# Pool matrix of whole numbers, pool channels as a high and a low part, in a two-layer hybrid encoder on one core

## The reference, cut to what matters

```python
for gi, w in enumerate(POOL_WINDOWS):        # 2, 4, 8, 16; one per group of 128 channels
    lo = jnp.clip(t - w // 2, 0, s)
    hi = jnp.clip(t + w - w // 2, 0, s)
    mean = (cs[:, hi, gi] - cs[:, lo, gi]) / (hi - lo)   # cs: cumulative sum over tokens
    outs.append(mean - uf[:, :, gi])
mixed = jnp.einsum('bsgc,gcd->bsgd', pooled, lin)        # one 128x128 map per group
return mixed.reshape(b, s, POOL_WIDTH) * scale
```

## Time and profile before

| | us |
|---|---|
| median of 3 runs | 810.91 (810.03 to 812.22) |
| the profiled execution, its own time | 810.14 |
| its span | 808.3 |
| TensorE busy | 802.1 |
| TensorE weight loads | 658.5 |
| VectorE busy | 572.9 |
| ScalarE busy | 464.0 |
| GpSimd busy | 245.9 |

### The profile page before, as it was taken

The page is one execution under the profiler, slowest core; times in us unless marked ns, Lnnn a source line. Parts: engine busy times, 40 slices in busy tenths (PEclk is TensorE's granted clock), DMA queues, the critical chain, the costliest instruction groups (busy, mean ns, idle before and its releaser), DMA issues.

```text
span 808.3 us, 9803 instructions
## 1 busy us (share of the span) xinstructions
PE 802.1 (99%) x3808; PEld 658.5 (81%) x3808; DVE 572.9 (71%) x684; ACT 464.0 (57%) x534; POOL 245.9 (30%) x206
## 2 busy tenths in 40 slices
PE   8999999999999999999999999999999999999998
PEld 6888877888888888888888887878888888888886
DVE  5899976758685666665379998777686666676551
ACT  5788886574355445544457888856635455355420
POOL 1342623330043444430023325342300444344200
PEclk9999999999999999999999999999999999999999
DMA  9788876864557787686456888675744666776651
GB/s 336 285 242 217 216 225 216 215 223 161 171 211 210 212 220 218 202 244 217 163 203 201 223 226 215 214 222 190 234 156 167 222 207 208 231 234 201 206 205 53
DMA packets 98318, 170.22 MB, mean 211 GB/s; under 512 B 78016, under 2 KB 78176, under 8 KB 80864
## 3 DMA queue, kind: packets, MB, share of 16 engines
q1 hardware_dynamic: 96352, 163.34, 65.5%
q0 software_dynamic: 1632, 6.18, 2.2%
q10 hardware_dynamic: 288, 0.08, 0.0%
HBM read 149.91 MB, written 1.05 MB: 187 GB/s over the span
## 4 chain that ended last, share of the span: by engine, by line
PE 97%; DVE 1%; DMA 1%; ACT 0%; SPq 0%; issue 0%
PE bank L1135 31%; PE bank L1146 30%; PE bank L1137 30%; PE bank L1257 2%; PE bank L1168 1%; PE bank L1234 1%; PE bank L1225 1%; PE bank L1195 1%; DMA x_sb<-in_x_dram 1%; PE bank L1201 0%; DVE w_lo L854 0%; DVE w_lo L860 0%; ACT w_hi L658 0%; DVE scratch L878 0%; DVE aT_lo L887 0%; ACT aT_hi L670 0%
## 5 line engine op out<-in xcount | busy, mean ns | idle before, releaser
L854 DVE TENSOR_TENSOR w_lo<-w_raw,w_hi 128x2048 fp32r<-128x2048 f32 x134 | 314.6, 2349 | 122.5 <-ACT w_hi L658 121.9
L658 ACT ACTIVATE w_hi<-w_raw 128x2048 fp32r<-128x2048 f32 x134 | 256.5, 1915 | 170.3 <-DMA w_raw<-in_stream_dram 170.3
L1135 PE MATMUL bank<-w_hi,aT_hi 128*128 128x512 f32 x832 | 327.6, 394 | 0.2 <-issue 0.2
L1137 PE MATMUL bank<-w_hi,aT_lo 128*128 128x512 f32 x832 | 324.1, 390 | 0.0
L1146 PE MATMUL bank<-w_lo,aT_hi 128*128 128x512 f32 x832 | 223.3, 390 | 0.2 <-DVE w_lo L854 0.2
L1135 PEld LDWEIGHTS bank<-w_hi,aT_hi 128*128 128x128 f32 x832 | 156.2, 188 | 36.6 <-issue 3.4
L1146 PEld LDWEIGHTS bank<-w_lo,aT_hi 128*128 128x128 f32 x832 | 155.6, 188 | 33.0 <-DVE w_lo L854 0.7
L1137 PEld LDWEIGHTS bank<-w_hi,aT_lo 128*128 128x128 f32 x832 | 156.3, 188 | 31.9
L597 POOL COPY halves<-hid 128x512 uint16<-128x512 uint16 x44 | 75.1, 1734 | 4.6 <-DVE hid L1107 4.6
L606 POOL COPY hT_raw<-turned 128x512 uint16<-128x512 uint16 x44 | 33.8, 813 | 134.4 <-DMA turned<-halves 134.4
L1135 PE MATMUL bank<-w_hi,hT_hi 128*128 128x512 f32 x176 | 68.6, 390 | 0.0
(11 more groups left out here) (102 smaller groups left out, 801.6 us busy)
## 6 DMA issues: line engine op xcount, KB each, us to landing
w_raw<-in_stream_dram SPq DMA_DIRECT2D x135, 1024.0 KB, 5.2
bias_sb<-in_b_gate_dram POOLq DMA_DIRECT2D x12, 256.0 KB, 5.7
par<-in_params_dram POOLq DMA_DIRECT2D x3, 384.0 KB, 3.4
w_raw<-in_stream_dram SPq DMA_DIRECT2D x4, 256.0 KB, 5.0
pool_mat<-in_pooling_dram POOLq DMA_DIRECT2D x1, 1024.0 KB, 5.2
out_dram<-x_sb SPq DMA_DIRECT2D x4, 256.0 KB, 3.9
x_sb<-in_x_dram SPq DMA_DIRECT2D x2, 256.0 KB, 4.6
x_sb<-in_x_dram SPq DMA_DIRECT2D x1, 512.0 KB, 7.0
```

Source lines behind the costliest of these rows:

```text
L658: nc.scalar.activation(w_hi[:, j % RING, :, :].rearrange("p k n -> p (k n)"), w_raw[:, j % RING, :, :].rearrange("p k n -> p (k n)"), ACT. ...
L854: nc.vector.tensor_tensor(w[0], w[1], w[2].bitcast(F32), ALU.subtract).then_inc(unit_lo, 1)
L1135: nc.tensor.matmul(o, src[0][:, k, tok], w_hi[:, slot, wk + i, :], start=first and i == 0, stop=False)
L1137: nc.tensor.matmul(o, src[1][:, k, tok], w_hi[:, slot, wk + i, :], start=False, stop=False)
```

## The change

The pool's matrix holds whole numbers: 1 in the window, less the window's count on the diagonal. It is kept as fp32r, cast once by GpSimd in units 7 and 8 of layer 0 from a raw copy that lands in the room of `head_halves`. The pool channels are taken from PSUM as a high part (`u_hi`, ScalarE, unit 13) and a low part (`u_lo`, VectorE, the new `low_pooled`, unit 15), each scaled by `rstd`. A turn is now eight fp32r matmuls in place of four fp32 ones. The turns move to units 16 and 18, z6 moves to banks 2 and 3, and is freed by `low_pooled`. The division by the count comes behind the per-group map: in the mixed turns VectorE multiplies by `pool_scale` and by 1/count in one instruction per group. The reciprocals are a new input, broadcast by one DMA per layer to `inv_counts`, issued by GpSimd in unit 17.

```diff
+U_LOW = 15
...
-    14: [("pool", 0)], 16: [("pool", 1)], 17: [("o", 0)], 20: [("o", 1)], 21: [("mixed", 0)], 23: [("mixed", 1)],
+    16: [("pool", 0)], 17: [("o", 0)], 18: [("pool", 1)], 20: [("o", 1)], 21: [("mixed", 0)], 23: [("mixed", 1)],
...
-        pair(2 if c in (0, 2, 4) else 0, f"z{c}")
+        pair(2 if c in (0, 2, 4, 6) else 0, f"z{c}")
...
-        pool_mat = sb("pool_mat", [P, MT, POOL_G, SEQ])
+        pool_mat = sb("pool_mat", [P, MT, POOL_G, SEQ], F32R)
...
+        pool_raw = head_halves[:, 0:MT * MT * POOL_G * SEQ].bitcast(F32)
...
-            zvu = sb("zvu", [P, MT, VU_W], F32, mixer)
+            zvu = sb("zvu", [P, MT, VU_POOL], F32, mixer)
+            u_hi = sb("u_hi", [P, MT, POOL_W], F32R, mixer)
...
+        inv_counts = zqk[:, 0, 1024:1024 + POOL_G * SEQ].rearrange("p (g n) -> p g n", g=POOL_G)
+        u_lo = [mixT_lo[:, 2:4, :].rearrange("p k n -> p (k n)"), oT_hi[:, 4:6, :].rearrange("p k n -> p (k n)")]
...
+            def load_counts(lay):
+
+                wait_joined(pool, lay, (5, 0))
+                pool.dma_start(inv_counts.rearrange("p g n -> p (g n)"), counts.to_broadcast([P, POOL_G * SEQ])
+                               ).then_inc(counts_loaded, 16)
+
...
-                    pool.dma_start(pool_mat[:, :, :, :].rearrange("p m g n -> p (m g n)"), pooling
+                    pool.dma_start(pool_raw, pooling
                                    ).then_inc(pooling_loaded, 16)
...
+                    if lay == 0 and t in (7, 8):
+                        m = t - 7
+                        pool.wait_ge(pooling_loaded, 16)
+                        for h in range(2):
+                            nc.gpsimd.tensor_copy(
+                                pool_mat[:, m, 2 * h:2 * h + 2, :],
+                                pool_raw.rearrange("p (m g n) -> p m g n", m=MT, g=POOL_G)[:, m, 2 * h:2 * h + 2, :]
+                                ).then_inc(pooling_ready, 1)
+                    if t == 17:
+                        load_counts(lay)
...
+                if c == POOL_CHUNK:
+                    nc.scalar.activation(u_hi[:, m, :], B((f"z{c}", m))[:, :], ACT.Copy, scale=rstd[:, 0, m:m + 1]
+                                         ).then_inc(pool_hi, 1)
+                    return
...
                 if kind == "mixed":
-                    gain = par[:, PR_PS + 2 * i:PR_PS + 2 * i + 2].unsqueeze(2).to_broadcast([P, 2, SEQ])
-                else:
-                    first = (PR_MIX if kind == "mix_x" else PR_FFN) + UK * (i // 2)
-                    gain = par[:, first:first + UK].unsqueeze(2).to_broadcast([P, UK, P])
+                    dve.wait_ge(counts_loaded, lay * 16 + 16)
+                    for h in range(2):
+                        g = 2 * i + h
+                        ins = nc.vector.scalar_tensor_tensor(
+                            scratch[:, NC * (n % 2) + SEQ * h:NC * (n % 2) + SEQ * h + SEQ],
+                            B(name)[:, SEQ * h:SEQ * h + SEQ], par[:, PR_PS + g:PR_PS + g + 1], inv_counts[:, g, :],
+                            ALU.mult, ALU.mult)
+                    free(ins, name)
+                    return
+                first = (PR_MIX if kind == "mix_x" else PR_FFN) + UK * (i // 2)
+                gain = par[:, first:first + UK].unsqueeze(2).to_broadcast([P, UK, P])
...
+            def low_pooled(lay, m):
+
+                for r, k in ((1, 0), (1, 1), (2, 0)):
+                    dve.wait_ge(heads_turned[r][k], (lay + 1) * 16)
+                dve.wait_ge(pool_hi, lay * MT + m + 1)
+                free(nc.vector.scalar_tensor_tensor(u_lo[m], B((f"z{POOL_CHUNK}", m))[:, :], rstd[:, 0, m:m + 1],
+                                                    u_hi[:, m, :].bitcast(F32), ALU.mult, ALU.subtract),
+                     (f"z{POOL_CHUNK}", m))
...
                     for j in splits_at(t):
                         split(lay, j)
+                    if t == U_LOW:
+                        for m in range(MT):
+                            low_pooled(lay, m)
...
-                        pe.wait_ge(pooling_loaded, 16)
+                        pe.wait_ge(pooling_ready, 2 * MT)
                         for m in range(MT):
                             wait_emptied(pe, lay, (f"z{POOL_CHUNK}", m))
                     for g in (2 * i, 2 * i + 1):
                         for m in range(MT):
-                            last = nc.tensor.matmul(b[:, SEQ * (g % 2):SEQ * (g % 2) + SEQ],
-                                                    zvu[:, m, VU_POOL + P * g:VU_POOL + P * g + P],
-                                                    pool_mat[:, m, g, :], start=(m == 0), stop=(m == MT - 1))
+                            for h, u in enumerate((u_hi[:, m, P * g:P * g + P], u_lo[m][:, P * g:P * g + P])):
+                                last = nc.tensor.matmul(b[:, SEQ * (g % 2):SEQ * (g % 2) + SEQ], u,
+                                                        pool_mat[:, m, g, :], start=(m == 0 and h == 0),
+                                                        stop=(m == MT - 1 and h == 1))
...
+    counts = np.zeros((1, POOL_G, SEQ), np.float32)
     for g, w in enumerate((2, 4, 8, 16)):
         for n, t in enumerate(flat):
             lo, hi = max(t - w // 2, 0), min(t + w - w // 2, SEQ)
             inside = (flat >= lo) & (flat < hi)
-            pool[inside, g, n] = np.float32(1.0) / np.float32(hi - lo)
-            pool[n, g, n] -= np.float32(1.0)
+            pool[inside, g, n] = np.float32(1.0)
+            pool[n, g, n] -= np.float32(hi - lo)
+            counts[0, g, n] = np.float32(1.0) / np.float32(hi - lo)
```

More of the change, by code:

```diff
@@ L221, in splits_at, with build @@
     return [t + 2] if t + 2 < UNITS else []
-def build(nc, x, stream, params, b_gate, eye, angles, pooling, mask, out):
+def build(nc, x, stream, params, b_gate, eye, angles, pooling, mask, counts, out):
     stream_v = stream.rearrange("u p n -> (u p) n")
@@ L313, in build @@
         pooling_loaded = sem("pooling_loaded")
+        pooling_ready = sem("pooling_ready")
+        pool_hi = sem("pool_hi")
+        pool_lo = sem("pool_lo")
+        counts_loaded = sem("counts_loaded")
         mask_loaded = sem("mask_loaded")
@@ L1370, in constants @@
             np.where((q - tok[m][None, :]) % 16 == 0, 0.0, NEG_INF)], 1))
-    return {"eye": eye, "angles": rope, "pooling": pool, "mask": np.concatenate(masks, 1).astype(np.float32)}
+    return {"eye": eye, "angles": rope, "pooling": pool, "mask": np.concatenate(masks, 1).astype(np.float32),
+            "counts": counts.reshape(1, POOL_G * SEQ)}
 def weight_stream(w_in, w_branch_a, w_branch_b, w_branch_c, w_out, w_ffn_gate, w_ffn_up, w_ffn_down):
```

## The result

The changed kernel takes 818.04 us (median of 6 runs, 815.68 to 819.34), the kernel before, on the same chip, 810.45 (also 6 runs): a ratio of 1.0087 [1.0074 to 1.0100]. It is slower, as forecast, but by 7.6 us and not by 2.5; the time lies above the range. The profiled run is the slowest of the six, 819.34 us with a span of 817.5 and a mean granted clock of 0.993; a run with 0.997 took 815.68.

The account below looks back on a forecast made before the run. TensorE's stream was taken to bound the kernel. Two waits of `values` totalling 5.68 us, less 3.20 us gained on the pool's products, gave +2.48 us and a median of 813.4 us, range 810.5 to 816.8 (8 in 10).

Parts of the forecast that it names:

- The pool's products: TensorE's four pool turns: each load and matmul pair at 0.116 us instead of 0.216, 3.20 us gained.
- Rival 2: Pool turns: load and matmul don't overlap at 256 columns, 817.0 us; weaker form 816.6; chance 0.16 with that form.
- The place of the wait and its chain: Unit 16: `values` waits for bank 2, freed by `low_pooled` behind `split(17)` and unit 17's load; 5.68 us over both layers.
- Rival 1: Unit 16: bank 2 is free in time, so no wait and all 3.2 us stays, 807.7 us; chance 0.11.
- What was taken at zero: Side work on VectorE, ScalarE, GpSimd and the queues, such as casts, counts' DMA and halved multiplies: no added time.
- At most 1.2 us: Upper bound for GpSimd's four casts in units 7 and 8 of layer 0, which were themselves taken at zero.
- z8 on bank 0: Bank 0 needed at 106.1 behind `values`, gates of z7 ending at 105.5 in layer 0: taken as zero cost.
- the size of the wait: TensorE's wait ahead of `values` in unit 16: 2.15 us in layer 0 and 3.53 in layer 1.
- landing less 3.1 us: Rule for each layer's wait at `values`, from unit 17's load time, 5.26 and 6.65 us.
- nearer 5.2 than 6.6: Where most landings of the stream were said to lie; 0.26 of the forecast's cases put over 813.3.
- Rival 3: Unit 16: the gap lowers TensorE's clock to 1.2 GHz for one unit, 5.44 us more, 818.8 us; chance 0.07.
- unit 18's early load: Issued 1.7 us earlier while unit 17's is under way; it can lengthen 17's landing or shift the long one between layers.

Follow-up runs that it names:

- e1: Changed kernel with `low_pooled` ahead of `split(17)` in VectorE's unit 15: 811.65 us, ratio 1.0016.
- e5: Changed kernel with SP issuing unit 17's load ahead of the transposes of the probabilities in unit 13: 809.39 us, ratio 0.9979.
- e2: Kernel before with only the pool's turns moved to units 16 and 18, products still fp32, same banks: 813.21 us, ratio 1.0036.
- e4: Changed kernel with 16 extra matmuls of 512 columns, result unused, on TensorE ahead of `values` in unit 16: 816.13 us, ratio 1.0067.
- e3: Changed kernel with SP holding unit 18's load, and the transposes of heads behind it, until unit 17's load has landed: 818.75 us, ratio 1.0090.
- e6: Changed kernel with unit 17's load ahead of the transposes and `low_pooled` ahead of `split(17)`: 808.28 us, ratio 0.9965.
- e8: Kernel before with only the SP edit, unit 17's load ahead of the transposes: 810.48 us, ratio 0.9993.
- e9: Kernel before with the turns in units 16 and 18 and unit 17's load ahead of the transposes, products still fp32: 810.58 us, ratio 0.9992.

## Why the prediction was wrong

- *The pool's products: right.* 0.119 us a pair against 0.116, so 3.1 us gained against 3.2. (The four loads named for 0.227, from 92.63 to 93.56, are 0.23 apart; 0.227 stands in other stretches. It changes nothing.) Rival 2 is refuted: the sum of load and matmul would have been 0.23. The Trainium skill, "TensorE: Matmul & The Clock Gate", lists in "Packing small matmuls — row/col tiling" that a weight load overlaps running matmuls only when the row groups differ; these rows don't bear that out either. The same section also lets a load be pulled ahead when it goes to the background weight buffer, which the prediction didn't weigh.
- *The place of the wait and its chain: right.* The first load of `values` in unit 16 starts 0.11 and 0.12 us behind the end of `low_pooled(0)`, which starts directly behind `split(17)`, in both layers. e1 takes this wait away by breaking one link, and e5 shortens it to 1.30 and 1.13 by breaking another. Rival 1 would have needed an earlier chain, and e5 shows what such a chain brings: 809.39.
- *What was taken at zero:* nothing else in TensorE's stream of the changed kernel waits longer than it did, and the counts' DMA and the halved multiplies cost nothing that can be seen. The casts on GpSimd do: 6.87 us where 2.2 stood, and 1.21 us of slowed VectorE rows, which in layer 0 of the profiled run, as far as the rows tell, end in the late load of the next point. "At most 1.2 us" was right; zero was not. One wait stayed hidden: z8 on bank 0 needs the gates of z7, 1.4 us behind `low_pooled`. The prediction had bank 0 wanted at 106.1, behind a late `values`, and so 0.6 us of room behind the gates at 105.5. That room exists only while `values` is late: without the first wait (e1, e2) the second opens, and in the changed kernel it stayed hidden.
- *The step that failed: the size of the wait.* "None of this hangs on the turn in unit 14, so it stays where it is" took the landings of one execution, 5.26 and 6.65 us, as they were. They came out at 7.56 and 6.8, and in layer 0 the load left 6.15 us behind unit 14's scores, not 5.0. The waits were 5.66 and 3.74 where 2.15 and 3.53 stood: +3.7 of the profiled run's miss of 6.7 (819.34 against 812.6). The forecast's own rule, landing less 3.1 us, with the late issue, gives 7.56 - 3.1 + 1.15 = 5.6: the rule held, its inputs didn't. The late issue goes with VectorE's delay beside the casts, shown above. Over the 12 landings of the kernels with this queue order (5.2 to 7.7, median 6.6) one of the two of before was the shortest and the other at the median, and the forecast's "nearer 5.2 than 6.6" came from all loads of the stream, most of which have no transposes ahead of them.
- *Rival 3, given 0.07, came true on top of that.* It was priced at 5.44 us for a whole unit at 1.2 GHz, for one layer. It was about 3.3 us in the profiled run over both layers (2.77 and 0.5), and 1.9 in the medians by e4, for a part of the low stretch lies in the gap, where TensorE has nothing to do. The forecast's own wait of 3.53 us lies between the gap of 3.27 that kept the clock and the one of 3.91 that lost it (e3), so 0.07 was far too little for it. The miss in the wait alone would have ended near the upper end of the range: e4, with most of the clock's share gone, stands at 816.13, and the forecast's 813.4 with 3.7 us added at 817.1. The two together make 818.04.
- *Shown and only argued.* Shown: the order on VectorE, the order on SP's queue, and that the clock has a share (its size roughly). Refuted: unit 18's early load as the main cause of the late landing, since holding it back gained nothing. A load ahead of the transposes lands in 4.8 to 5.6 us (8 loads in e5, e6, e8, e9), one behind them in 5.2 to 7.7. Why it is slower there is open. So is why two of the twelve took over 7.5 (layer 0 of the changed kernel and of e4): both left late, with unit 18's load 1.6 us behind, which e3 didn't have; a third such load (e4, layer 1) landed in 5.8. Only argued: that the casts made the load of layer 0 late. Their 1.21 us is in the rows, and without it VectorE would have stood 3.5 us behind the scores, where e2 and e3 stood with their joins on time (3.4); no run took the casts out of the changed kernel.

## What to carry to other kernels

When a consumer of a bank moves to another engine, list what stands in that engine's order ahead of the new instruction, back to the DMA that feeds it, and look which instruction of the bound engine meets it; here the loss could be undone in two places in program order, one on VectorE and one on SP's queue, and swapping both turned 7.6 us lost into 2.7 gained. Size a wait that ends in a DMA's landing by the landings of all executions and layers with the same queue in front, at their upper end, and not by the one that the trace shows. Count a forecast gap on TensorE with its slowed matmuls behind it. And don't put new work on an idle engine at zero before asking whom it slows beside it: the casts on GpSimd made VectorE's instructions longer, and by these rows the delay went on to SP's queue.

## What the runs showed of the hardware

- The granted clock fell to 1.2 GHz with gaps of 6.01 and 4.09 us (after) and 3.91 (e3, layer 1), and also with 2.45 us behind 16 filling matmuls (e4, layer 0). It stayed at 1.00 with gaps of 3.27 (e3, layer 0), 2.33 (e2, layer 1) and 2.16 (e1, layer 0). So in these rows a gap's length alone does not tell.
- In the longest gap the clock fell inside the gap. In the shorter ones it fell when TensorE was at work again: `values` started at 509.07 and the window from 508 to 510 still reads 0.94; in e4 it started at 107.51 and the window to 108 reads 1.00. The slowed stretch then lies wholly in work, so the shorter gap isn't cheaper: 1.15 us of slowed `values` and 0.5 of slowed matmuls behind 4.09, 1.62 of slowed `values` behind 6.01.
- fp32r products of 256 columns with a full load each run at 0.119 us, about half of the 512-column pitch of 0.227, with load and matmul overlapped.
- A 1 MB load issued right behind the DMA transposes took 5.2 to 7.7 us to land, one issued ahead of them 4.8 to 5.6. The neighbours differ as well: ahead of the transposes it leaves some 5 or 6 us earlier, long before unit 18's load. With unit 18's load held back (e3) it still took 5.9 and 6.6.
- VectorE's instructions took longer while GpSimd cast beside them: 1.10 us for 0.68, 2.69 for 2.28, 1.12 for 0.74. Of GpSimd's four casts of 128x512 the two that began beside VectorE's splits took 2.67 us each, the others 1.07 and 0.61.
